# The last expert block's down matrices in three parts, and the overflow branch ahead of that block's last work

## The chip, the cores and the metric

The kernel runs on one NeuronCore of a Trainium2 chip. TensorE multiplies matrices and transposes, VectorE and ScalarE work elementwise, GpSimd gathers rows, SyncE issues most transfers; each has its own instruction stream, and they meet only at semaphores. Sixteen DMA engines move data between HBM and the on-chip memory. The metric is the time of one execution on the device in microseconds (us); smaller is better.

## The reference

Two transformer layers on 512 tokens of width 1024, in float32. Layer 0 has differential attention, layer 1 dilated attention over three groups. Each layer then has a mixture of experts, and this is what matters here: 32 experts in 4 groups, two experts for each token, each expert a gated network with a hidden width of 512.

```
g_idx = argmax(h @ w_group + b_group);  gates = g_w * softmax(top2 of the group's 8 experts)
expert(xb, e) = (silu(xb @ w_gate[e]) * (xb @ w_up[e])) @ w_down[e]
y[token] += gate * expert(h[token], e)
x = x + g_f * y
```

The gate and up matrices are 1024 x 512 and a down matrix is 512 x 1024, 2 MB each. Every expert's three matrices are read in both layers.

## The kernel before

After the routing, the (token, expert) pairs stand sorted into 14 blocks (NB) of 128 rows. Experts are ranked by load. The first blocks hold one expert each (WIDE), then come blocks that hold two experts of 64 rows (PAIRS) and blocks that hold four experts of 32 rows (FOURS). COLS says in which order the blocks are worked; the last one, block 13 in order, is a block of four experts. What doesn't fit in these rows would go through an overflow pass: a flag holds by how much an expert is overfull, and every engine branches on it. With this case's data the flag is zero and the pass is jumped over. Its code stands there all the same.

For a block p, TensorE does gate_up(p) (two products, each over 8 slices of the contraction), hidden_t(p) (four transposes of HIDDEN), down(p) and token_sums(p). In down(p) the product goes through two halves of the output columns (hf), and within each through 4 slices k of the contraction. For a block of four experts the four quarters run side by side in four column groups of the array, so 2 x 4 x 4 matmuls. A float32 matmul is two records in the trace, so they are 64 records. VectorE multiplies silu(gate) by up (hidden, L1497), copies the transposes (hidden_t, L1503), scales each half of the result into Y (y_out, L1519), and adds the token sums to x (add_sum, L1530). token_sums(p) (L2221) brings the rows of Y back to their tokens: eight matmuls of 128 x 512, for two halves and four chunks of tokens.

The order of the matrices is written out in MOE_ORDER: gate and up of a block, then down of the block before; for the last two blocks down of block 12, gate and up of block 13, down of block 13. SyncE issues them in that order, all on one queue (L529). Each goes to a fixed slot (8 slots in layer 0, 9 in layer 1), and SyncE first waits until the slot's last user is done. The slot's semaphore says when the matrix has arrived; TensorE waits for it in arrived().

At the end of a layer TensorE's order is: gate_up(13), hidden_t(13), down(13), the load of the flag and the branch (L2241), token_sums(13). VectorE's order is: pick, hidden, hidden_t and y_out of block 13, the flag and the branch (L1560), the eight additions. ScalarE branches at L995, GpSimd at L649, SyncE at L533, after the last down matrix is issued. Behind the additions of layer 0 follow the squares and the transposes of layer 1's attention, behind those of layer 1 the output.

Of the kernel before, what the change touches and what calls it, by code (L numbers as in the profile page):

```python
# [15 lines left out]
P = 128  # L16
# [209 lines left out]
def program(nc, t, const, masks, buckets, out):  # L226
    with ExitStack() as ctx:
# [193 lines left out]
        XR = [V[:, D * i:D * (i + 1)] for i in range(2)]  # L421
        HIDDEN, HIDDEN_T = V[:, 4 * D:4 * D + HALF], V[:, 4 * D + HALF:5 * D]
        Y = V[:, 5 * D:6 * D]
        PICK = [W[:, 2048:2560], W[:, 512:1024]]
        TOKENS = W[:, 2560:3072]

# [10 lines left out]
        def _(sp):  # L437
# [35 lines left out]
            for l in range(LAYERS):  # L473
                for n, (kind, layer, i) in enumerate(ORDER):
                    if layer != l or kind == "moe":
                        continue
                    if kind == "mod":
                        load(n, columns(t["kv_ada_w"], i - 12) if 12 <= i < 16 else
                             columns(t["ada_w"][i // 16], i % 16))
                    elif kind == "v":  # L480
                        load(n, columns(t["a_w_qkv"][0], 4 + i) if l == 0 else columns(t["kv_w"], GROUPS + i))
                    elif kind == "kq":
                        slot_free(n)
                        if l == 0:
                            parts = [(t["a_w_qkv"][0], D + 2 * P * i), (t["a_w_qkv"][0], 2 * P * i)]
                        else:
                            hh, g = divmod(i, GROUPS)
                            parts = [(t["kv_w"], g * HALF + hh * 2 * P), (t["b_w_q"][0], g * HALF + hh * 2 * P)]
                        for to, (w, at) in enumerate(parts):
                            sp.dma_start(slot(n)[:, 2048 * to:2048 * (to + 1)].rearrange("p (k n) -> p k n", k=KC),  # L490
                                         w[:, at:at + 2 * P].rearrange("(k p) n -> p k n", p=P)).then_inc(w_in[SLOT[n]], 16)
                    elif l == 0:
                        load(n, columns(t["a_w_o"][0], i))
                    else:
                        load(n, t["b_w_o"][0].rearrange("(k p) n -> p k n", p=P), k=4)

                m = AT["moe", l, 0]
                expert, ranked = {}, False
                for i, (p, kind, half) in enumerate(MOE_ORDER):  # L500
                    r = rank_of(p, half)
                    if r < FIXED:
                        expert[r] = r
                    elif kind == "g":
                        if not ranked:
                            sp.wait_ge(*sm[l]["eid_ready"](1))
                            ranked = True
                        expert[r] = sp.value_load(eid[0:1, r:r + 1], min_val=0, max_val=E - 1)
                    g, u, d = expert_weights(l, expert[r])
                    if l == 1 and i == 2:  # L510
                        sp.wait_ge(*sm[1]["qk_pe"](N_TILES))
                    elif l == 1 and i == 3:
                        sp.wait_ge(*sm[1]["s_pe"](N_STEPS))
                    elif l == 1 and i == 4:
                        sp.wait_ge(*sm[1]["pt_pe"](N_STEPS))
                    if i == 5:
                        sp.wait_ge(*sm[l]["gath"][0](16))
                    if SLOT[m + i] == RING and PREVIOUS[m + i] is None or l == 1 and i == 5:
                        if l == 0:
                            sp.wait_ge(t1_copy, 3)  # L520
                        sp.wait_ge(*sm[l]["xn_out"](16))
                        sp.wait_ge(*sm[l]["route_pe"](2))
                    elif (l, i) in ((0, 7), (1, 6)):
                        sp.wait_ge(*sm[l]["wo_pe"](2 * TC))
                    elif l == 1 and i == 7:
                        sp.wait_ge(*sm[1]["y_added"](2 * TC))
                        sp.wait_ge(*sm[1]["gate_pe"](2))
                    slot_free(m + i)
                    sp.dma_start(slot(m + i), {"g": g, "u": u, "d": d}[kind]).then_inc(w_in[SLOT[m + i]], 16)  # L529
                    if kind == "d":  # L530
                        del expert[r]

                most = sp.value_load(flag[0:1, 0:1], min_val=0, max_val=S)  # L533
                with sp.If(most > 0):
                    sp.wait_ge(*sm[l]["dn_pe"](2 * NB))
                    for b in range(OV_ROUNDS):
                        with sp.Fori(0, E) as e:
                            u0 = b * E
                            g, u, d = expert_weights(l, e)

                            sp.wait_ge(*ov[l]["dn_pe"](e + u0))
                            sp.dma_start(slot(0), g).then_inc(ov[l]["w"].sem, 16)
                            sp.dma_start(slot(1), u).then_inc(ov[l]["w"].sem, 16)
                            sp.dma_start(slot(2), d).then_inc(ov[l]["w"].sem, 16)
                    sp.wait_ge(*ov[l]["dn_pe"](OV_ROUNDS * E))
                    sp.wait_ge(*ov[l]["scat"](64 + 16 * OV_ROUNDS * E))
                    for c in range(TC):
                        if c:
                            sp.wait_ge(*ov[l]["hid"](OV_ROUNDS * E + c))
                        sp.dma_start(V[:, 0:2 * D].rearrange("p (k n) -> p k n", k=2), rows_of(l, c)).then_inc(ov[l]["w"].sem, 16)  # L550
                    sp.wait_ge(*ov[l]["hid"](OV_ROUNDS * E + TC))
# [461 lines left out]
        def _(dve):  # L1013
# [28 lines left out]
            for l in range(LAYERS):  # L1042
# [504 lines left out]
                y_out(NB - 2)  # L1547
                add_sums(NB - 2)
                pick(NB - 1)
                hidden(NB - 1)  # L1550
                hidden_t(NB - 1)
                y_out(NB - 1)

                def add_rows(c, signal, at):
                    step(dve.tensor_tensor(x3[:, c, :], x3[:, c, :], at[:, 0:D], ALU.add))
# [3 lines left out]

                most = dve.value_load(flag[0:1, 0:1], min_val=0, max_val=S)  # L1560
                with dve.If(most > 0):
                    for bb in range(OV_ROUNDS):
                        if bb:
                            dve.wait_ge(*o["tab_pe"](bb))
                        rows_at = ov_row[:, A * bb:A * (bb + 1)]
                        main_step, step = step, Steps(dve, o["step_dve"].sem)
                        step.base = bb if bb == 0 else bb + 2
                        step(dve.tensor_scalar(rows_at, over_by, float(-QP - P - P * bb), None, ALU.add))
                        if bb == 0:
                            step(dve.tensor_copy(OHW[:, :, 0:E], OHS))  # L1570
                            step(weigh(OHW, E))
                            dve.tensor_tensor(OHW[:, :, 0:E], OHW[:, :, 0:E], ids(E), ALU.mult)
                        step = main_step
                        for a in range(A):
                            at = 2048 + a * P
                            ins = dve.tensor_scalar(W[:, at:at + P], C[:, C_IOTA:C_IOTA + P], rows_at[:, a:a + 1], None, ALU.is_equal)
                        ins.then_inc(o["tab_f"].sem, 1)
                        dve.wait_ge(*o["tab_pe"](bb + 1))
                        cols = slice(bb * E, (bb + 1) * E)
                        main_step, step = step, Steps(dve, o["step_tab"].sem)  # L1580
                        step.base = 2 * bb
                        slot_table(bank[2][:, 0:2 * E], E, gate_ov[:, cols], dst_ov[:, cols], tok_ov[:, cols], o["tok"].sem, 3072 - 64)
                        step = main_step
# [18 lines left out]
                        add_rows(c, o["hid"].sem, V[:, 0:2 * D])  # L1602
                    dve.wait_ge(*o["hid"](OV_ROUNDS * E + TC))
                    step = main_step

                for c in range(TC):
# [16 lines left out]
        def _(pe):  # L1624
# [43 lines left out]
            for l in range(LAYERS):  # L1668
# [559 lines left out]
                for p in range(NB):  # L2228
# [4 lines left out]
                    elif p == NB - 2:  # L2233
                        down(p)
                        token_sums(p)
                        gate_up(p + 1)
                    else:
                        hidden_t(p)
                        down(p)

                most = pe.value_load(flag[0:1, 0:1], min_val=0, max_val=S)  # L2241
                with pe.If(most > 0):
                    pe.wait_ge(*s["y_evac"](2 * NB))
                    ohs = W[:, 0:4 * TC * E].rearrange("p (a n) -> p a n", n=2 * E)
                    for bb in range(OV_ROUNDS):
# [8 lines left out]
                    for bb in range(OV_ROUNDS):  # L2254
                        with pe.Fori(0, E) as e:
# [24 lines left out]
                                                    start=(k == 0), stop=(k == 3))  # L2280
                            ins.then_inc(o["dn_pe"].sem, 1)
                    pe.wait_ge(*o["y"](2 * OV_ROUNDS * E))

                token_sums(NB - 1)

# [31 lines left out]
```

## Time and profile before

| | us |
|---|---|
| three runs, median | 1838.29 |
| lowest, highest | 1838.28, 1844.95 |
| the profiled execution | 1839.16 |
| its span, first to last instruction | 1837.3 |
| TensorE busy | 1674.6 (91%) |
| VectorE busy | 653.2 (36%) |
| ScalarE busy | 371.1 (20%) |
| GpSimd busy | 55.3 (3%) |

A record is one instruction of one execution, in us from the span's start. PE is TensorE, PEld its loading of weights, DVE VectorE, ACT ScalarE, POOL GpSimd, SP SyncE; a q behind the name means the engine's sequencer. Busy time of a group counts overlapping records once. PEclk is the share of full clock that TensorE was granted: 1.00 is 2.4 GHz, 0.50 is 1.2 GHz.

### The profile page before, as it was taken

The page shows a single profiled execution, that of the slowest core. Times are in us where ns is not written, and L with a number is a line of the kernel's source. Part 1 is how long each engine was busy: PE and PEld are TensorE (multiplying, and loading weights), DVE is VectorE, ACT ScalarE, POOL GpSimd, SP SyncE. Part 2 cuts the span into 40 slices and gives each one's busy share as a digit, 9 for nine tenths or more (in the row PEclk, how much of TensorE's full clock was granted, in tenths as well). Part 3 has the DMA queues.
Part 4 walks back from the last instruction along what each step waited for, and adds up shares of the span by engine and source line. Part 5 has one row for each costly group of instructions (what it writes and reads, how often), then busy time and mean ns, then how long its engine had stood idle before and what let it go on. Part 6 is the DMA issues. An engine that isn't in the chain of part 4 may idle for free.

```text
span 1837.3 us, 18111 instructions
## 1 busy us (share of the span) xinstructions
PE 1674.6 (91%) x6904; PEld 732.1 (40%) x6904; DVE 653.2 (36%) x1400; ACT 371.1 (20%) x916; POOL 55.3 (3%) x61
## 2 busy tenths in 40 slices
PE   5999999988998997998699999998889989979995
PEld 2455555443332332332244455444433323323331
DVE  2576654350322322323376122224522322322331
ACT  3124344221111010010210143333311101001000
POOL 1000000210000000000000000001000000000000
PEclk9999998999999998999899999999999999989998
DMA  9962722149999999999666112021199999999995
GB/s 356 349 238 83 274 92 92 50 182 404 427 427 427 426 428 425 428 426 408 229 217 196 45 46 92 0 92 50 46 374 427 426 426 427 425 427 427 428 426 223
DMA packets 102524, 523.30 MB, mean 285 GB/s; under 512 B 6836, under 2 KB 44165, under 8 KB 77854
## 3 DMA queue, kind: packets, MB, share of 16 engines
q1 hardware_dynamic: 77632, 484.46, 64.6%
q0 software_dynamic: 7392, 19.99, 3.0%
q10 hardware_dynamic: 17406, 17.59, 3.0%
q8 instruction: 60, 0.98, 0.2%
q14 instruction: 34, 0.28, 0.0%
HBM read 521.98 MB, written 6.32 MB: 288 GB/s over the span
## 4 chain that ended last, share of the span: by engine, by line
PE 80%; DMA 11%; DVE 5%; issue 2%; ACT 1%; ACTq 0%; SPq 0%; DVEq 0%
PE psum L2177 19%; PE psum L2208 11%; PE psum L2221 10%; PE psum L1720 9%; PE psum L1928 9%; DMA ring<-in_moe_w_up_dram 6%; PE psum L1898 3%; PE psum L1775 3%; PE psum L2153 2%; DMA XN<-in_moe_w_up_dram 1%; DVE W L1077 1%; DMA XN<-in_moe_w_down_dram 1%; DMA HT<-in_moe_w_down_dram 1%; DMA V<-xn_scratch,tok 1%; PE psum L1749 1%
## 5 line engine op out<-in xcount | busy, mean ns | idle before, releaser
L2177 PE MATMUL psum<-ring,V 128*32 128x512 f32 (+2 forms) x1440 | 354.4, 619 | 31.0 <-DMA ring<-in_moe_w_up_dram 11.5
L2221 PE MATMUL psum<-V,W 128*128 128x512 f32 x448 | 220.3, 618 | 9.4 <-issue 4.6
L2208 PE MATMUL psum<-ring,V 128*64 128x512 f32 (+2 forms) x752 | 206.1, 609 | 20.7 <-DMA HT<-in_moe_w_down_dram 9.9
L2177 PEld LDWEIGHTS psum<-ring,V 128*32 128x32 f32 (+2 forms) x1440 | 118.6, 137 | 207.5 <-issue 201.1
L1530 DVE TENSOR_TENSOR X<-X,psum 128x512 f32<-128x512 f32 x224 | 153.7, 687 | 71.3 <-PE psum L2221 71.3
L972 ACT ACTIVATE V<-psum,modall,scls 128x128 f32<-128x128 f32 x216 | 81.1, 456 | 332.4 <-PE psum L2153 332.4
L1077 DVE SCALAR_TENSOR_TENSOR W<-ring,cact,W 128x512 f32<-128x512 f32 (+1 forms) x224 | 138.5, 618 | 7.7
L2221 PEld LDWEIGHTS psum<-V,W 128*128 128x128 f32 x448 | 73.0, 190 | 155.3 <-DVE X L1530 85.3
L2177 PE MATMUL psum<-XN,V 128*32 128x512 f32 (+2 forms) x240 | 112.6, 625 | 22.4 <-DMA ring<-in_moe_w_up_dram 22.1
L2177 PE MATMUL psum<-HT,V 128*32 128x512 f32 (+2 forms) x256 | 117.8, 615 | 3.5 <-DMA ring<-in_moe_w_up_dram 3.2
L1720 PE MATMUL psum<-HT,ring 128*128 128x512 f32 x256 | 117.2, 605 | 0.0
L1519 DVE SCALAR_TENSOR_TENSOR V<-psum,slot_gate,W 128x512 f32<-128x512 f32 x56 | 42.0, 751 | 207.3 <-PE psum L2208 207.3
L981 ACT ACTIVATE V<-psum 128x512 f32<-128x512 f32 x28 | 16.7, 597 | 486.3 <-PE psum L2186 405.2
L1497 DVE TENSOR_TENSOR V<-V,psum 128x512 f32<-128x512 f32 x28 | 19.2, 687 | 264.6 <-PE psum L2177 264.6
L2208 PEld LDWEIGHTS psum<-ring,V 128*64 128x64 f32 (+2 forms) x752 | 64.3, 138 | 121.4 <-issue 121.4
L1928 PE MATMUL psum<-HT,ring 128*128 128x512 f32 x192 | 88.8, 607 | 0.0
L1928 PE MATMUL psum<-ring 128*128 128x512 f32 x192 | 87.1, 596 | 0.0
L1503 DVE COPY V<-psum 128x512 f32<-128x512 f32 x28 | 19.4, 691 | 174.2 <-PE psum L2186 174.2
L1720 PEld LDWEIGHTS psum<-HT,ring 128*128 128x128 f32 x256 | 48.1, 193 | 56.2 <-issue 55.8
L1243 DVE SCALAR_TENSOR_TENSOR ring<-psum,colV,W 128x512 f32<-128x512 f32 x24 | 23.7, 989 | 112.5 <-ACT W L860 112.5
L2208 PE MATMUL psum<-XN,V 128*32 128x512 f32 (+1 forms) x128 | 61.2, 626 | 0.0
L1720 PE MATMUL psum<-ring,HT 128*128 128x512 f32 x128 | 59.1, 612 | 0.0
(313 smaller groups left out, 1822.7 us busy)
## 6 DMA issues: line engine op xcount, KB each, us to landing
ring<-in_moe_w_gate_dram SPq DMA_DIRECT2D x49, 2048.0 KB, 24.1
ring<-in_moe_w_down_dram SPq DMA_DIRECT2D x47, 2048.0 KB, 23.9
ring<-in_moe_w_up_dram SPq DMA_DIRECT2D x41, 2048.0 KB, 22.8
ring<-in_ada_w_dram SPq DMA_DIRECT2D x16, 2048.0 KB, 15.4
HT<-in_moe_w_up_dram SPq DMA_DIRECT2D x10, 2048.0 KB, 23.8
XN<-in_moe_w_gate_dram SPq DMA_DIRECT2D x9, 2048.0 KB, 21.7
XN<-in_moe_w_down_dram SPq DMA_DIRECT2D x8, 2048.0 KB, 21.6
ring<-in_ada_w_dram ACTq DMA_DIRECT2D x16, 1024.0 KB, 5.3
```

What stands on the lines that cost most here:

```text
L972: ins = act.activation(V[:, 2 * D + b * D + k * P:2 * D + b * D + (k + 1) * P], bank[0][:, q * P:(q + 1) * P], ACT.Identity, bias=mod[:, 2 ...
L1077: ins = dve.scalar_tensor_tensor(acc, w[:, k, :], cact[:, k:k + 1], acc, ALU.mult, ALU.add)
L1519: dve.scalar_tensor_tensor(Y[:, cols], bank[6 + hf], slot_gate[:, COLS[p]:COLS[p] + 1], gf_row[:, cols], ALU.mult, ALU.mult).then_inc(s["y ...
L1530: return dve.tensor_tensor(x3[:, c, cols], x3[:, c, cols], sum_bank(p, hf, c), ALU.add)
L1720: ins = pe.matmul(bank[n % 2], rows, cols, start=(k == 0), stop=(k == KC - 1))
L1775: ins = pe.matmul(bank[WO_BANKS[0][u]], OT0[k][:, c * P:(c + 1) * P], w3[:, k, :], start=(k == 0), stop=(k == KC - 1))
L1898: ins = pe.matmul(bank[u % 4], rows, slot3(n)[:, k, :], start=(k == 0), stop=(k == KC - 1))
L1928: ins = pe.matmul(bank[n % 2], w[:, k, (hp % 2) * P:(hp % 2 + 1) * P], (HTQ if kind else ht3)[:, k, :], start=(k == 0), stop=(k == KC - 1))
L2153: ins = pe.transpose(to[:, q * P:(q + 1) * P], V[:, b * D + k * P:b * D + (k + 1) * P], ident)
L2177: ins = pe.matmul(bank[2 + 2 * i + b][half * w:(half + 1) * w, :], V[:, col:col + w], slot3(x)[:, k, :], start=(k == 0), stop=(k == KC - 1))
L2208: ins = pe.matmul(bank[6 + hf][half * w:(half + 1) * w, :], HIDDEN_T[:, col:col + w], slot3(x, 4)[:, k, hf * HALF:(hf + 1) * HALF], start= ...
L2221: pe.matmul(sum_bank(p, hf, c), PICK[p % 2][:, c * P:(c + 1) * P], Y[:, hf * HALF:(hf + 1) * HALF], start=True, stop=True).then_inc(s["sum ...
```

## The change

The down matrices of block 13 come in three parts: columns 0 to 2D of the slot (slices k = 0 and 1) of all four experts, then slice 2 of all four, then slice 3 of all four. The first parts signal the slots' semaphores, the others two new ones, d_rest. TensorE's new last_down does hidden_t, then eight matmuls of ones into bank 0 whose result nobody uses, waits for the transposed rows, and goes through the three parts; in each part both halves of the columns. Both halves are finished in the last part. The flag is loaded and the branch taken before last_down on TensorE, and before hidden, hidden_t and y_out of block 13 on VectorE; so these stand in both arms of the branch.

```diff
+        d_rest = [sem("d_rest0"), sem("d_rest1")]
+        LAST_DOWN = ((0, 1), (2,), (3,))
...
-                    sp.dma_start(slot(m + i), {"g": g, "u": u, "d": d}[kind]).then_inc(w_in[SLOT[m + i]], 16)
-                    if kind == "d":
+                    if kind == "d" and p == NB - 1:
+                        sp.dma_start(slot(m + i)[:, 0:2 * D], d[:, 0:2 * D]).then_inc(w_in[SLOT[m + i]], 16)
+                    else:
+                        sp.dma_start(slot(m + i), {"g": g, "u": u, "d": d}[kind]).then_inc(w_in[SLOT[m + i]], 16)
+                    if kind == "d" and p < NB - 1:
                         del expert[r]
+                for part, rest in enumerate(d_rest):
+                    cols = slice((2 + part) * D, (3 + part) * D)
+                    for half in range(halves(NB - 1)):
+                        n = m + MOE_AT[NB - 1, "d", half]
+                        d = expert_weights(l, expert[rank_of(NB - 1, half)])[2]
+                        sp.dma_start(slot(n)[:, cols], d[:, cols]).then_inc(rest, 16)
...
                 pick(NB - 1)
-                hidden(NB - 1)
-                hidden_t(NB - 1)
-                y_out(NB - 1)
+
+                def last_rows():
+                    hidden(NB - 1)
+                    hidden_t(NB - 1)
+                    y_out(NB - 1)
...
                 with dve.If(most > 0):
+                    last_rows()
...
+                with dve.Else():
+                    last_rows()
...
-                    else:
-                        hidden_t(p)
-                        down(p)
+
+                def last_down():
+
+                    p, n = NB - 1, halves(NB - 1)
+                    w = P // n
+                    hidden_t(p)
+                    for _ in range(8):
+                        pe.matmul(bank[0], ones, C[:, 0:512], start=True, stop=True)
+                    at = [m + MOE_AT[p, "d", half] for half in range(n)]
+                    pe.wait_ge(*s["hid_t"](p + 1))
+                    pe.wait_ge(*s["y_evac"](p * 2))
+                    for part, ks in enumerate(LAST_DOWN):
+                        if part == 0:
+                            for x in at:
+                                arrived(pe, x)
+                        else:
+                            pe.wait_ge(d_rest[part - 1], 16 * n * (l + 1))
+                        for hf in range(2):
+                            for k in ks:
+                                for half, x in enumerate(at):
+                                    col = k * P + half * w
+                                    ins = pe.matmul(bank[6 + hf][half * w:(half + 1) * w, :], HIDDEN_T[:, col:col + w],
+                                                    slot3(x, 4)[:, k, hf * HALF:(hf + 1) * HALF],
+                                                    start=(k == 0), stop=(k == 3))
+                            if part == 2:
+                                ins.then_inc(s["dn_pe"].sem, 1)
 
                 most = pe.value_load(flag[0:1, 0:1], min_val=0, max_val=S)
                 with pe.If(most > 0):
+                    last_down()
...
+                with pe.Else():
+                    last_down()
 
                 token_sums(NB - 1)
```

## Rows read from the trace of the kernel before

**Rows 1.** Waits, 1790 to 1838: who waited for whom: us in total, times, longest

```profile
PE psum L2208 <- DMA XN<-in_moe_w_down_dram: 9.7, 1, 9.7
PE psum L2177 <- DMA ring<-in_moe_w_up_dram: 3.2, 1, 3.2
```

**Rows 2.** Chain of waits, end of layer 1: start, us, what

```profile
1792.29 21.61 DMA XN<-in_moe_w_down_dram
...
1814.40 8.97 PE psum L2208 x64
...
1824.97 7.12 PE psum L2221 x16
```

**Rows 3.** Waits, 850 to 900

```profile
PE psum L2208 <- DMA HT<-in_moe_w_down_dram: 9.9, 1, 9.9
...
PE psum L2221 <- issue: 4.6, 1, 4.6
```

**Rows 4.** Timeline, end of layer 0: start, us, engine line op, what, count [idle before]

```profile
856.14 0.81 SPq L529 DMA_DIRECT2D ring<-in_moe_w_down_dram  x2
...
859.36 8.59 PE L2177 MATMUL psum<-ring,V 128*32 128x512 f32 x64 [3.28 <-DMA ring<-in_moe_w_up_dram]
868.00 12.97 SPq L465 DMA_DIRECT2D ring<-in_kv_w_dram  x3
...
892.78 8.80 PE L2221 MATMUL psum<-V,W 128*128 128x512 f32 x16 [4.57 <-issue]
...
907.18 2.82 PE L1862 MATMUL psum<-C,XN 128*128 128x128 f32 x12 [5.59 <-DVE XN L1057]
```

**Rows 5.** Timeline, end of layer 1

```profile
1802.55 0.60 PE L2177 MATMUL psum<-ring,V 128*32 128x512 f32 x3
...
1804.03 0.66 PE L2186 MATMUL psum<-C,V 128*128 128x128 f32 x4 [0.88 <-DVE V L1497]
...
1818.42 0.61 PE L2208 MATMUL psum<-ring,V 128*32 128x512 f32 x3
...
1819.71 0.61 PE L2208 MATMUL psum<-ring,V 128*32 128x512 f32 x3
...
1820.03 0.75 DVE L1519 SCALAR_TENSOR_TENSOR V<-psum,slot_gate,W 128x512 f32<-128x512 f32 x1 [14.62 <-PE psum L2208]
...
1822.71 0.61 PE L2208 MATMUL psum<-ring,V 128*32 128x512 f32 x3
```

**Rows 6.** Instructions of L2241, both layers: count, ns min/median/max, first and last start

```profile
L2241 PEldq TENSOR_LOAD <-flag x2: 315/404/492, 885.5 to 1820.6; - x2
...
L2241 PEldq SEQ_ASSERT  x2: 18/23/28, 886.2 to 1821.2; - x2
```

**Rows 7.** DMA queues, 890.00 to 890.25: queue, kind: packets, MB, share

```profile
q8 instruction: 1, 0.02, 27.5%
```

**Rows 8.** DMA queues, 1822.25 to 1822.50

```profile
q8 instruction: 1, 0.02, 28.9%
```

**Rows 9.** Instructions of L995 (ScalarE's branch), 1780 to 1800

```profile
L995 ACTq SEQ_ASSERT  x1: 18/18/18, 1791.9 to 1791.9; - x1
```

**Rows 10.** DMA queues, 1795.5 to 1796.0

```profile
q14 instruction: 1, 0.01, 3.9%
```

**Rows 11.** DMA queues, 893.25 to 893.50

```profile
q8 instruction: 1, 0.02, 31.9%
```

**Rows 12.** Windows: stretch, length, busy of five engines, PEclk, DMA share, GB/s

```profile
1812.00:1813.00 1.00, 0.00 (x0) 0.00 (x0) 0.00 (x0) 0.00 (x0) 0.00 (x0) 0.50 0.19 82
...
1800.00:1805.00 5.00, 3.80 (x36) 1.19 (x28) 0.97 (x2) 0.00 (x0) 0.00 (x0) 1.00 1.01 433
887.00:888.00 1.00, 1.00 (x12) 0.14 (x4) 0.00 (x0) 0.00 (x0) 0.00 (x0) 1.00 1.05 387
893.00:894.00 1.00, 1.00 (x2) 0.39 (x2) 0.00 (x0) 0.00 (x0) 0.00 (x0) 0.59 0.90 307
895.00:900.00 5.00, 5.00 (x11) 2.20 (x10) 3.00 (x5) 0.16 (x1) 0.00 (x0) 0.84 0.01 2
```

## The prediction

> **What bounds the kernel now.** I read the chain of waits first: 80% of the span is TensorE. So what matters of the change is where it touches that chain, at the end of each layer's expert work. I then read the waits of those two stretches. In layer 1 TensorE sits 9.7 us in front of the last down products, until the last matrix lands, and 3.2 us in front of the up products [rows 1]. The chain of that tail [rows 2] is one piece after the other: transfer until 1813.9, down products from 1814.40, token sums from 1824.97, the last additions, output. Layer 0 looks the same, with a wait of 9.9 us, plus one that layer 1 has not: 4.6 us of "issue" ahead of the token sums [rows 3], where nothing that the profile names is late. The two timelines [rows 4, 5] give the places. The reader is to see that the last-landing transfer and the work behind it (9 us of down products, a branch, sums) stand in series in both layers.
>
> **Branch before the sums, as it is.** TensorE's sequencer loads the flag at 885.5 (layer 0) and 1820.6 (layer 1) [rows 6], 2.1 us before it starts its last down matmul (1822.71 in layer 1). The first sum starts at 892.78 and 1824.97 [rows 4, 2]. From load to first matmul: 7.3 us and 4.35 us. Why they differ shows in the instruction packets: the sequencer is ready at 886.2 and 1821.2 [rows 6]; the 16 KB packet of code follows at 890.0 and 1822.25 [rows 7, 8], so after 3.8 us and 1.0 us; the first matmul comes 2.7 us behind the packet in both. In layer 0 the transfer engines were full then (share 1.05, [rows 12]), in layer 1 empty. ScalarE's own branch in layer 1, taken at 1791.9 beside full engines [rows 9], has its packet at 1795.5, again 3.6 us [rows 10]. So a branch that needs a code block fetched costs 7.3 us beside full transfers and 4.35 us beside idle ones.
>
> **Part 1, the branch goes ahead of the last work.** Now the flag is loaded behind the last up matmul. That one starts at 859.36 + 8.59 - 0.59 = 867.36 in layer 0 and 1802.55 in layer 1 [rows 4, 5]. Less 2.1 us: loads at 865.3 and 1800.45. Both places lie inside the down transfers, with engines full (1.01, 433 GB/s, [rows 12]). I take 7.3 us for both; the other bound is 4.35 us. The first transposes of HIDDEN start at 872.6 and 1807.75. Without a branch they started at 1804.03 in layer 1 [rows 5], so 3.7 us are lost here, which would be hidden under the transfer if nothing followed. The other engines' branches: VectorE's moves behind the pick of block 13, some 18 us ahead of its next work; SyncE's stays last but follows 12 issues in place of 4, at about 0.42 us each (two took 0.81 us, [rows 4]), done by 861.2, while its next transfer waits until 868.00 anyway.
>
> **Part 2, eight warming matmuls.** They stand between the transposes and the wait for the matrices, of the same shape as the eight token sums (16 records of 128x512). Those took 7.12 us in layer 1 and 8.80 us in layer 0 [rows 2, 4], where TensorE had stood 4.6 us and the granted clock then fell to 1.2 GHz (0.59 in the second microsecond, [rows 12]). In the changed kernel TensorE stands 4.7 us, until 872.6 and 1807.75. So I take 8.8 us; with the clock kept it is 7.1. Behind 0.6 us of transposes they run 873.2 to 882.0 and 1808.35 to 1817.15.
>
> **Part 3, matrices in three parts.** The last byte comes no earlier. Four 2 MB transfers become four of 1 MB (8 KB per partition) and eight of 0.5 MB (4 KB), in one queue. The trace has full engines with 16 KB pieces at 433 GB/s and 2 KB pieces (layer 1's first weights) at 387 [rows 12]. Bounds for the last landing: 0 and 8.39 MB/387 - 8.39 MB/433 = 2.3 us later. I take 0.6 us, nearer the large pieces: 880.0 and 1815.0. Starvation is excluded: the pieces are issued faster (0.42 us) than they run (1.2 to 2.4 us). The first part, half the bytes, is in before 1806 and before 871. TensorE comes to it at 882.0 and 1817.15, when in layer 0 and in layer 1 all three parts have landed. Hence **no wait for a matrix is left: TensorE itself sets the end**, through the branch and the warming matmuls, and splitting the products gains only that they don't start cold.
>
> The products are 64 records in 16 passes of four; a pass at 2.4 GHz is (1822.71 - 1818.42)/10 = 0.43 us [rows 5], so 6.9 us in place of 8.97. They end at 888.9 and 1824.05. The first half of Y is ready only two passes before the end: its last matmul starts at 887.6, VectorE follows 0.3 us later and takes 0.75 [rows 5], done at 888.65. That is the one thing the split takes away (it used to be done 2.7 us before the end), and the last two passes still cover it. At 1.2 GHz it would be covered too.
>
> **Sum.** Layer 0: sums start at 888.9 in place of 892.78, 3.9 us earlier, and run warm, 7.1 in place of 8.8, 1.7 us more: 5.6 us. Layer 1: 1824.05 in place of 1824.97, 0.9 us. Behind the sums everything keeps its distance: in layer 0 the next transposes (907.18, waiting for VectorE) follow the additions, and the weights they meet are in since 895 (share 0.01, [rows 4, 12]). Layer 1 of the network starts 5.6 us earlier and ends 6.5 us earlier. The profiled execution took 1839.16 us: 1832.7. The median of the three runs shown, 1838.29, lies 0.9 us below it: 1831.8. I say 1832.
>
> Does each transfer cost something of its own? Five microseconds in which one down matrix ends and the next begins show 433 GB/s and share 1.01, with no hole [rows 12]. The Trainium skill (DMA: Bandwidth & Descriptors, "Bandwidth") asks for transfers of at least 1 MiB and its section on the anatomy of a DMA charges about 2.0 us for each. If that were paid in series, eight more would put the last landing 16 us later and the whole at some 1851; the trace does not agree, it shows such a cost only once, behind the last byte.
>
> **Rivals.**
> A, the fetch is cheap or the clock stays. If the branch costs 4.35 us, as beside idle transfers, layers 0 and 1 each start 2.95 us earlier; if the clock holds over the then shorter stand, 1.7 us more each. Both: 6.5 + 2 x 4.65 = 15.8, 1823. One of them: 1826 to 1829. For it: in layer 0 the last landing (880.0) would still be early enough, since the third part would be asked for at 882.5 at the earliest. Against: the two branches seen beside full engines, TensorE's and ScalarE's, waited 3.8 and 3.6 us for their packets. 25%.
> C, transfers pay by number. From the last bytes (within 1812 to 1813, [rows 12]) to the first product at 1814.40 pass about 1.6 us. Eight more transfers in series: 12.8 us, last landings at 892.2 and 1827.2. With 1.8 to 3.4 us of products behind them sums start at 894.0 and 1830.5, so 1.2 and 5.5 later, 1845. It decides from 8 us of delay on, for TensorE is not ready before. The full share above speaks against it. 4%.
> D, layer 0's gain is not passed on and only layer 1's 0.9 us stay: 1837.4. Against it the 12 us between the last weight's landing and its use. 7%.
> The forecast has the remaining 52%.
>
> **How the numbers follow.** The forecast's own spread is 1829 to 1835: 0.6 us of landing does nothing, the clock in one of the two layers does 1.7, runs differ by a microsecond. To hold 8 in 10 I go down to 1824, which leaves out only the fullest form of A, and up to 1839, which takes in D and the light half of B. What a measurement of this kernel can tell from no change is 0.5%, 9.2 us. Faster by more: most of A, and a forecast that errs by 3 us: 0.27. Slower by more: the heaviest B and what I don't see: 0.06. Within: 0.67.
>
> **What would show it.** In the changed profile: TensorE's flag load near 865 and 1800 minus the shift; its packet about 3.8 us behind; first transposes 7.3 us behind the load; 16 records of warming taking 8 to 9 us; no idle TensorE between them and the products; products 7 us, warm; sums directly behind, 7.1 us in both layers; the last landing earlier than the last part is asked for. It is wrong if TensorE waits again for a down matrix, if the load-to-transpose distance is under 5 us or over 9, or if a gap appears within the products.

## The result, and the profile after

| | before | after |
|---|---|---|
| median of 20 runs, us | 1840.40 | 1846.01 |
| lowest, highest | 1836.70, 1845.06 | 1841.63, 1848.29 |
| profiled execution, us (span) | 1839.16 (1837.3) | 1845.79 (1843.9) |
| first sum, layer 0 | 892.78 | 889.52 |
| last addition, layer 0 | 901.76 | 897.19 |
| block 13's hidden, layer 1 | 1803.28 | 1803.91 |
| first sum, layer 1 | 1824.97 | 1830.98 |

The ratio is 1.0029, interval 1.0020 to 1.0039: 5.3 us slower (3.7 to 7.2). 1832 with a range of 1824 to 1839 was forecast; the sign was wrong. Both profiles lie near their medians, so the 6.6 us between them can be followed through: layer 0 ends 4.6 us earlier, as forecast; the stretch from there to the end of layer 1 takes 5.2 us more (901.5 became 906.7); from hidden to the first sum of layer 1 are 27.1 us in place of 21.7, 5.4 more; the output 0.7 more.

**Layer 0** came as the sum had it. Timeline of TensorE and VectorE in the changed kernel (start, us; idle before and its releaser in brackets); the rows of before are [rows 4].

```profile
872.29 1.09 PE L2202 MATMUL psum<-C,V 128*128 128x128 f32 x4 [4.34 <-issue]
873.17 9.17 PE L2260 MATMUL psum<-C 128*128 128x512 f32 x16
...
889.52 7.11 PE L2237 MATMUL psum<-V,W 128*128 128x512 f32 x16 [0.18 <-DVE V L1530]
...
897.19 0.69 DVE L1541 TENSOR_TENSOR X<-X,psum 128x512 f32<-128x512 f32 x1 [0.35 <-issue]
```

The reader is to see the branch as "issue" (nothing that the profile names is waited for) ahead of the transposes (forecast 872.6), the sixteen slow records of warming (forecast 8.8 us), and sums that run at 2.4 GHz, 7.11 us for 8.80. The flag's load stands where it should, 7.1 us ahead of the first transpose:

```profile
L2280 PEldq TENSOR_LOAD <-flag x2: 315/403/491, 865.2 to 1801.0; - x2
```

**Layer 1** has the same pieces and one more. The chain of waits of the changed kernel (start, us, what); of before, [rows 2].

```profile
1796.70 7.11 PE psum L2193 x64
...
1803.91 0.70 DVE V L1508
1804.61 3.15 issue
1807.76 0.66 PE psum L2202 x2
1808.42 5.11 issue
1813.53 0.69 PE psum L2202 x2
1814.22 9.58 PE psum L2260 x16
1823.80 6.19 PE psum L2274 x56
...
1830.98 7.12 PE psum L2237 x16
```

The first "issue" is the branch. Then two records of transposes run, half of the four, and TensorE stands again for 5.11 us with nothing to wait for. In that time the next packet of its code travels; DMA queues of the changed kernel, 1810.75 to 1811.00:

```profile
q1 hardware_dynamic: 27, 0.10, 98.6%
q8 instruction: 1, 0.02, 27.2%
```

Read with e1 and e5 below: the branch landed a few records before the end of a code block, the next block was asked for only then, beside full transfers, and work resumed 2.6 us behind its packet, about the distance of [rows 7, 8] again. From there on the pieces are as forecast, and late. No down matrix is waited for: the waits of 1780 to 1850 hold no line with in_moe_w_down_dram.

**The middle.** Nothing of the change stands between 897 and 1795, and yet 5.2 us go there. Windows of 1240 to 1270, the end of layer 1's attention, where TensorE works in short pieces (the eighth figure is the granted clock): first before, then the changed kernel.

```profile
1240.00:1250.00 10.00, 6.92 (x49) 4.14 (x49) 3.63 (x11) 4.91 (x13) 0.00 (x0) 1.00 0.59 211
1250.00:1260.00 10.00, 7.38 (x92) 6.06 (x90) 7.73 (x25) 6.06 (x19) 4.92 (x5) 1.00 0.12 17
1260.00:1270.00 10.00, 7.65 (x34) 3.58 (x33) 2.50 (x4) 3.89 (x6) 0.00 (x0) 1.00 0.02 2
```

```profile
1240.00:1250.00 10.00, 6.91 (x60) 5.32 (x58) 4.45 (x18) 4.01 (x12) 0.00 (x0) 0.81 0.58 212
1250.00:1260.00 10.00, 7.65 (x70) 5.78 (x68) 7.67 (x22) 6.74 (x21) 4.91 (x5) 0.85 0.11 17
1260.00:1270.00 10.00, 8.34 (x29) 3.90 (x30) 1.53 (x3) 3.22 (x5) 0.00 (x0) 0.83 0.00 0
```

Before was granted 2.4 GHz throughout; the changed kernel does the same work partly at 1.2 GHz. (0.19 + 0.15 + 0.17) x 10 us = 5.1 us of clock missing, which is at most what it can cost here. It isn't the only place: from 900 to 910 the changed kernel was granted 0.66, the kernel before 0.84. Added up in such windows from 900 to 1330, the changed kernel spends 34 us at 1.2 GHz, the kernel before 20.

### The profile page after: what moved, and what is told of

It is laid out like the page before. It is cut to its first block, busy times and chain, and to the rows that moved or that the text cites. A ratio compares the mean times of both kernels' runs of the same rounds, so it can differ in the third digit from the quotient of the medians.

```text
span 1843.9 us, 18223 instructions
## 1 busy us (share of the span) xinstructions
PE 1695.1 (92%) x6936; PEld 743.1 (40%) x6936; DVE 653.4 (35%) x1400; ACT 371.5 (20%) x916; POOL 55.3 (3%) x61
## 4 chain that ended last, share of the span: by engine, by line
PE 80%; DMA 11%; DVE 5%; issue 2%; ACT 1%; SPq 1%; DVEq 0%
PE psum L2193 19%; PE psum L2224 10%; PE psum L1944 9%; PE psum L1736 9%; PE psum L2237 9%; DMA ring<-in_moe_w_up_dram 8%; PE psum L1914 3%; PE psum L1791 3%; PE psum L2169 2%; DMA XN<-in_moe_w_up_dram 1%; DVE W L1088 1%; DMA ring<-in_ada_w_dram 1%; PE psum L2049 1%; DMA V<-xn_scratch,tok 1%; PE psum L1765 1%
## 5 line engine op out<-in xcount | busy, mean ns | idle before, releaser
L2224 PE MATMUL psum<-ring,V 128*64 128x512 f32 (+2 forms) x672 | 188.3, 596 | 1.1 <-issue 1.0
L2193 PE MATMUL psum<-XN,V 128*32 128x512 f32 (+2 forms) x240 | 111.9, 621 | 21.1 <-DMA ring<-in_moe_w_up_dram 20.8
L1508 DVE TENSOR_TENSOR V<-V,psum 128x512 f32<-128x512 f32 x28 | 19.3, 688 | 264.1 <-PE psum L2193 264.1
L2224 PEld LDWEIGHTS psum<-ring,V 128*64 128x64 f32 (+2 forms) x672 | 59.4, 139 | 90.5 <-issue 90.5
L1944 PE MATMUL psum<-ring 128*128 128x512 f32 x192 | 87.0, 596 | 0.0
L1914 PE MATMUL psum<-ring 128*128 128x512 f32 x128 | 57.0, 598 | 0.0
```

What stands on the lines that cost most here:

```text
L1914: ins = pe.matmul(bank[u % 4], rows, slot3(n)[:, k, :], start=(k == 0), stop=(k == KC - 1))
L1944: ins = pe.matmul(bank[n % 2], w[:, k, (hp % 2) * P:(hp % 2 + 1) * P], (HTQ if kind else ht3)[:, k, :], start=(k == 0), stop=(k == KC - 1))
L2193: ins = pe.matmul(bank[2 + 2 * i + b][half * w:(half + 1) * w, :], V[:, col:col + w], slot3(x)[:, k, :], start=(k == 0), stop=(k == KC - 1))
L2224: ins = pe.matmul(bank[6 + hf][half * w:(half + 1) * w, :], HIDDEN_T[:, col:col + w], slot3(x, 4)[:, k, hf * HALF:(hf + 1) * HALF], start= ...
```

## The experiments

Two theories stood to be tested. **Landing**: the second stand in layer 1 made the change slow, and nothing else did. **Middle**: when layer 0 ends at another moment, other idle gaps of TensorE fall to 1.2 GHz, and some 5 us go that way in this kernel. The texts on record call them T and M; theory A in the later ones says that a delay costs its own length and nothing else. Each kernel below was compared with runs of the kernel before on the same chip; c1 is a single run. "Middle" is the distance in the profiled execution from the start of the last addition of layer 0 to hidden of block 13 in layer 1; "tail" that from there to the first sum.

| kernel | what it is | median, us | against before, us (interval) | last addition, layer 0 | middle | tail |
|---|---|---|---|---|---|---|
| before | | 1840.25 | | 901.76 | 901.5 | 21.7 |
| c1 | before once more | | | 902.09 | 901.7 | 21.5 |
| after | | 1846.01 | +5.3 (+3.7 to +7.2) | 897.19 | 906.7 | 27.1 |
| e1 | after, landing moved | 1840.27 | +0.2 (-2.4 to +2.6) | 896.60 | 906.5 | 21.1 |
| e2 | e1, branch late | 1833.03 | -7.9 (-11.4 to -4.4) | 895.08 | 905.0 | 16.8 |
| e3 | e1 without warming | 1829.34 | -11.6 (-16.0 to -7.4) | 891.41 | 907.0 | 15.0 |
| e4 | before, branch early | 1837.07 | -2.2 (-5.0 to +0.4) | 893.71 | 907.0 | 20.6 |
| e5 | e3, layer 0's gap filled | 1828.26 | -12.7 (-16.2 to -9.0) | 890.93 | 904.9 | 18.5 |
| e6 | before, held 1.1 us | 1845.69 | +6.6 (+4.0 to +9.0) | 901.61 | 907.8 | 21.9 |
| e7 | e3, branch between gate and up | 1823.81 | -17.3 (-21.0 to -13.6) | 887.94 | 905.8 | 15.3 |
| e8 | e7, held 2.2 us | 1822.38 | -15.3 (-19.3 to -11.4) | 891.79 | 902.1 | 14.6 |
| e9 | e7, layer 0's gap filled | 1820.74 | -18.9 (-21.3 to -16.4) | 892.26 | 900.1 | 14.7 |

The fourth column is the ratio of the comparison, less one, times the median of before on that chip (1840.40 for after, 1840.25 for e1 to e4, 1838.29 for e5 to e7, 1838.81 for e8 and e9). The last three are of one execution each. How far such an execution can stray shows in e7, e8 and e9: up to the first sum of layer 0 they hold the same code, and it starts at 880.24, 881.26 and 883.43.

**e1, the landing moved.** Records that never run, in the overflow arm, push the other arm along in the code:

```diff
                 with pe.If(most > 0):
+                    for _ in range(30):
+                        pe.matmul(bank[0], ones, C[:, 0:512], start=True, stop=True)
                     last_down()
```

> The changed kernel, with 30 matmuls (120 records) more in the overflow arm, which is never executed; all that changes is where TensorE's branch lands in its 16 KB code block. In the changed kernel's layer 1 two transposes run, then TensorE stands 5.1 us until the next code block is in. Theory T (landing): the stand goes, as 124 records are left behind the landing in place of some 4. Layer 1: transposes 1807.8 and all done, warming to 1817, products to 1824, sums at 1824.3 in place of 1830.98. So 6 to 7 us faster than the changed kernel in both theories. They part on the whole: T says that nothing but the stand made the change slow, so the gain of layer 0 (4.7 us) shows: some 7 us faster than before, 1833 to 1835 where before is 1840. Rival M (middle): between 902 and 1795 the changed kernel lost 8 us against before because what follows layer 0's earlier end doesn't keep up (other gaps get the slow clock), systematically; then this one is within 2 us of before.

(The middle's 8 us of this text are 5.2 by the profiles. And the padding stands in layer 0's arm too, whose code lies ahead of layer 1's, so how many records were left behind the landing isn't known from the edit.)

It came back to the time of before. The chain of e1's layer 1:

```profile
1803.75 3.05 issue
1806.80 1.09 PE psum L2202 x4
1807.88 9.04 PE psum L2260 x16
...
1824.10 7.12 PE psum L2237 x16
```

All four transposes run at once, no second stand, and the tail is 21.1 us for 27.1. So the second stand is worth 5.1 us by the ratios (1.0029 to 1.0001), 6.0 us in the profile: shown. But the theory that it was all fails: e1 ought to have been 7 us faster than before and is not. Layer 0 ends 5.2 us earlier, the tail is 0.6 us shorter, and the middle takes 4.9 us more.

**e2, the branch back behind the products.** last_down() and last_rows() stand once, ahead of the branches; parts and warming stay, and e1's padding too.

```diff
+                last_down()
                 most = pe.value_load(flag[0:1, 0:1], min_val=0, max_val=S)
                 with pe.If(most > 0):
-                    last_down()
...
-                with pe.Else():
-                    last_down()
```

> The changed kernel with the branches of TensorE and VectorE back behind the last products (three parts and warming kept; 120 unexecuted records in the overflow arm to keep the landing off a block's end). T: transposes at 868.8 and 1804.0, warming to 876.5 and 1811.7, products to 883.4 and 1818.6; then the branch, 7.3 us from load to sums in layer 0 and 4.35 in layer 1: sums at 888.6 and 1820.9 against 892.78 and 1824.97 before. 8 us faster than before. M: the layer 0 part (4 us) and more is lost again in the middle: within 2 us of before.

8 us faster than before, and so 8 us faster than e1, which differs in the place of the two branches alone (TensorE's and VectorE's). Where TensorE sets the end, the branch in front of the work costs more (7 us of fetching beside full transfers) than behind it (in layer 1 beside idle ones).

**e3, no warming.** The loop of eight matmuls is taken out of last_down, and 152 records stand in the overflow arm, to keep the landing clear of a block's end.

```diff
-                    for _ in range(8):
-                        pe.matmul(bank[0], ones, C[:, 0:512], start=True, stop=True)
```

> The changed kernel without the eight warming matmuls (and with 152 unexecuted records in the overflow arm, so that the landing is that of e1). T: the products begin behind the transposes at 874 and 1808.9, half of them at 1.2 GHz, and end with the last part: 882.5 and 1817.5. Sums 6.5 us earlier per layer than in e1, so 13 us faster than e1 and 18 to 20 faster than before: 1821. M: layer 0's share is lost, 7 us faster than e1. A rival W, that the warming pays for itself (products and sums cold without it): no faster than e1.

11 us faster than e1. Timeline of e3's TensorE in layer 1:

```profile
1802.27 0.63 PE L2202 MATMUL psum<-C,V 128*128 128x128 f32 x4 [4.04 <-issue]
1803.68 1.07 PE L2272 MATMUL psum<-ring,V 128*32 128x512 f32 x3 [0.78 <-DVE V L1514]
...
1813.38 7.11 PE L2237 MATMUL psum<-V,W 128*128 128x512 f32 x16
```

The products begin 1.4 us behind the transposes and take 9.7 us up to the sums, 2.5 us more than the changed kernel's 7.2 behind its warming, which had cost 9.0. Of these, 1.4 us are the slow clock (granted 0.86 over the 9.70) and 1.1 us a pause in the middle of a pass, which ends at 1807.89, 2.5 us behind a code packet at 1805.43: the landing wasn't quite that of e1. Rival W is out. The sum from the landing theory (18 to 20 us faster than before) is missed by the middle again, 907.0.

**e4, the early branch alone.** One transfer for each matrix, no warming, products half by half.

```diff
-        LAST_DOWN = ((0, 1), (2,), (3,))
+        LAST_DOWN = ((0, 1, 2, 3),)
...
-                            if part == 2:
+                            if True:
```

> The kernel before with the branch ahead of the last work alone: one transfer for each down matrix, products half by half, no warming (152 unexecuted records in the overflow arm). T: products start on arrival (879.4, 1814.4) as before and take 9 us cold, sums follow at once: 888.5 against 892.78 and warm (1.7 us less), 1823.5 against 1824.97. Some 7 us faster than before. M: within 2 us of before.

2.2 us faster, with an interval that just holds zero; 8 us earlier at the end of layer 0, and 5.4 us given back in the middle. Against e3 it also says what the three parts are worth: 9.4 us by the ratios, 7.7 by the medians. Its chain has the matrix and then all the products:

```profile
1790.43 22.27 DMA XN<-in_moe_w_down_dram
1812.71 0.14 issue
1812.84 8.51 PE psum L2263 x64
1821.35 7.08 PE psum L2228 x16
```

**c1, before once more.**

> The kernel before, unchanged, profiled a second time. From the last addition of layer 0 (901.65) to that of block 13's first VectorE work in layer 1 (1803.28) the first profile has 901.6 us; the changed kernel and the four variants have 905 to 907.5. Theory M (the middle loses 4 to 6 us whenever layer 0 ends earlier): 901 to 903 again, with about 20 us at 1.2 GHz between 900 and 1330. Rival L (the first profile was a lucky execution, the middle varies from run to run): somewhere else, 904 or more.

901.7 us, so two profiles of before agree, and the other five kernels' 905 to 907 stand apart from them. Both are of executions near the median, though (1839.2 and 1839.3). On this chip the runs of before go from 1836.1 to 1844.7 us, and the granted clock of the whole execution is 0.960 in the longest and 0.967 in the shortest: now and then before, too, loses some microseconds to the clock, and no profile shows where.

**e6, before, held back.** One more Square ahead of layer 1's first; it puts the real one 1.1 us later (899.12 to 900.21), not the 1.25 us that were expected.

```diff
                     junk = HT[:, 0:D] if l == 0 else W[:, 2048:2048 + D]
+                    if l == 1 and c == 0:
+                        act.activation(junk, x3[:, c, :], ACT.Square).then_inc(held, 1)
+                        act.wait_ge(held, 1)
```

> The kernel before with one more Square of 128x1024 on ScalarE (1.25 us) ahead of layer 1's first, which holds back the start of layer 1's attention by 1.25 us and changes nothing else. Additive theory A: 1.25 us slower than before, no more. Theory M in its clock form: which idle gaps of TensorE fall to 1.2 GHz depends on where they lie in time, so a shift of a microsecond can cost several: more than 3 us slower, with 29 us or more at 1.2 GHz between 900 and 1330 in place of 20.

**1.1 us of delay cost 6.6 us** (4.0 to 9.0), and theory A is out. The last addition of layer 0 starts at 901.61, as before; the tail is the same; the middle has 907.8. Part of the delay lies ahead of that addition, for VectorE first waits for a Square. A cleaner measure starts at layer 1's first transposes, behind the whole delay: from there to hidden are 896.1 us in before, 896.3 in c1 and 901.8 in e6, so 5.6 to 5.7 us are lost after the delay is over. Windows of e6:

```profile
1240.00:1250.00 10.00, 8.19 (x45) 4.53 (x43) 3.13 (x10) 4.25 (x13) 0.00 (x0) 1.00 0.56 200
1250.00:1260.00 10.00, 8.71 (x73) 7.24 (x72) 6.50 (x22) 5.73 (x20) 3.24 (x3) 0.66 0.03 12
1260.00:1270.00 10.00, 6.07 (x46) 3.92 (x45) 5.44 (x9) 3.86 (x6) 1.68 (x3) 0.88 0.12 17
```

This is the picture of the changed kernel, made from the kernel before by a delay alone. Over the whole stretch from 900 to 1330 the granted clock of before, and then of e6, is

```profile
900.00:1330.00 430.00, 403.08 (x1578) 203.20 (x1576) 177.28 (x431) 130.88 (x290) 9.42 (x8) 0.98 0.27 89
```

```profile
900.00:1330.00 430.00, 403.74 (x1554) 203.50 (x1553) 172.13 (x411) 130.05 (x288) 9.43 (x8) 0.96 0.27 89
```

that is some 20 us at 1.2 GHz against 34 (added up in windows of 10 us; the two decimals here leave 4 us either way).

**e5, the gap of layer 0's end filled.** Six matmuls of ones behind layer 0's token sums, into a bank that VectorE has read.

```diff
                 token_sums(NB - 1)
+                if l == 0:
+                    pe.wait_ge(*s["summed"](2 * TC * (NB - 1) + 1))
+                    for _ in range(6):
+                        pe.matmul(bank[2], ones, C[:, 0:512], start=True, stop=True)
```

> e3 with six matmuls of ones behind layer 0's last token sums, into a bank already read, so that TensorE stands 0.6 us in place of 5.8 before layer 1's first transposes. M (clock): the spell at 1.2 GHz at 895.1 to 901.9 goes, in which TensorE worked for 5.2 us, so 2.6 us are saved there; later spells may shift either way, so 0 to 6 us faster than e3. A: exactly 2.6 faster. If the clock has nothing to do with the middle's loss: no change from e3.

The middle fell by 2.1 us (904.9), near the 2.6 that theory A had for it, but the times (1 us apart, both intervals 7 to 9 us wide) don't tell it from nothing. The tail says why: 18.5 us for e3's 15.0. TensorE in layer 1, and the DMA queues from 1802.75 to 1803.00:

```profile
1799.76 0.63 PE L2202 MATMUL psum<-C,V 128*128 128x128 f32 x4 [4.11 <-issue]
...
1805.23 1.07 PE L2272 MATMUL psum<-ring,V 128*32 128x512 f32 x3 [2.13 <-issue]
```

```profile
q8 instruction: 1, 0.02, 27.1%
```

After the transposes and two passes of products TensorE stands for 2.13 us with nothing to wait for, a code packet travels, and work goes on 2.4 us behind it; the clock granted from there to 1810 is 0.50. The six matmuls lie ahead of layer 1's code and moved its landing nearer to a block's end. It is the changed kernel's second stand once more, brought in by an edit somewhere else, and with it e5 says nothing against the clock.

**e7, the branch where TensorE waits anyway.** The gate product is done, then the branch, then the up product in both arms.

```diff
-                        gate_up(p + 1)
+                        gate_up(p + 1, only=(0,))
...
                     w = P // n
+                    gate_up(p, only=(1,))
                     hidden_t(p)
```

> e3 with TensorE's branch between block 13's gate and up products, where TensorE waits for the up matrices anyway (both arms hold the up product too; the landing in the code block stays). In e3 the transposes stand 4.0 and 4.4 us behind hidden for the branch's sake. Here the flag is loaded 2.1 us before the gate product's end, the first up matmul comes 7.3 us later, so 5.2 us behind the gate product in place of 3.9 and 2.9: up products 1.3 and 2.3 us later, transposes 3.1 and 1.7 us earlier than in e3. If TensorE still sets the end, 3 and 1.7 us faster per layer than e3; if the last part's landing does by then, less. 0 to 5 us faster than e3.

5.5 us faster than e3, just above what was expected. Now the down matrices set the end at last; e7's chain:

```profile
1788.13 17.72 DMA XN<-in_moe_w_down_dram
...
1805.89 3.22 PE psum L2276 x16
1809.11 7.08 PE psum L2240 x16
```

Behind the last part only its sixteen records are left, which is what splitting along the contraction is for.

**e8 and e9, the best version.** e8 is e7 with two extra Squares as in e6; e9 is e7 with e5's six matmuls.

> e7, held back at the start of layer 1 by two extra Squares on ScalarE (2.5 us). e7 has the middle of the changed kernel (906 us from layer 0's last addition to block 13 in layer 1, three spells at 1.2 GHz at 1235, 1252 and 1262), the kernel before has 901.7 and one spell there. Additive theory A: 2.5 us slower than e7. Theory M in its clock form: the delay moves the idle gaps again; the loss may vanish, then the middle is 901.7 + 2.5 at most and the run 0 to 3 us faster than e7 in spite of the delay; or it stays, then 2.5 us slower. Either M outcome must agree with the spells in its profile.

> e7 with six matmuls of ones in TensorE's gap behind layer 0's last token sums, as e5 was to e3. e5 was 1 us faster than e3 by the medians, where the spell of its gap alone was worth 2.6. A: 2.6 us faster than e7. M: between 1 us slower and 5 us faster, by where the later gaps fall. This and e8 are the two candidates for the best version.

In e8 the loss of the middle vanished: 902.1 us, where e7 has 905.8. From layer 1's first transposes, behind the delay (2.2 us here), it is 896.6 for 900.5. Its windows (against 0.81 and 0.85 in the changed kernel):

```profile
1240.00:1250.00 10.00, 7.38 (x91) 6.06 (x92) 7.72 (x25) 6.06 (x19) 4.93 (x5) 1.00 0.12 18
1250.00:1260.00 10.00, 7.64 (x36) 3.87 (x35) 2.96 (x5) 3.90 (x6) 0.00 (x0) 1.00 0.02 1
```

So the delay did not make it slower beyond doubt: the medians put e8 1.4 us ahead of e7, the ratios 2 us behind, and the intervals overlap. e9 has the shortest middle of all, 900.1 us (894.8 from the first transposes), and is the fastest kernel run: 0.9897 of before (0.9884 to 0.9911), 1820.74 us, and by the ratios some 24 us faster than the changed kernel.

## Why the prediction was wrong

- **The branch's price** (7.3 us beside full transfers, for both layers): right. Load to first transpose is 7.1 us in layer 0 (865.2 to 872.29) and 6.8 in layer 1 (1801.0 to 1807.76). Rival A was wrong.
- **The warming matmuls** (8.8 us, and TensorE, not the matrices, sets the end): right, 9.2 and 9.6 us. The prediction saw that they take the place of the wait that the parts remove, and e3 confirms it: without them 11 us less.
- **The parts**: their last landing stayed ahead of TensorE's need; rival C was wrong. The landing was to come 0.6 us later. From the last up matrix's landing to the last down's are 20.5 us for 19.8 in layer 0, so 0.6 it was, but in layer 1 21.5 (1796.57 to 1818.12) for 19.5 (1794.38 to 1813.89), 2.0 us later and within the bound of 2.3; it cost nothing here, as TensorE came to it at 1823.8. The 2.0 us for each transfer that the prediction weighed stand in the Trainium skill (DMA: Bandwidth & Descriptors, "Anatomy of one DMA — SWDGE (gpsimd) path") for transfers that GpSimd issues; these are SyncE's. Products 7.1 us in layer 0 (882.27 to 889.35) where 6.9 stood, no gap in them.
- **Layer 0's 5.6 us**: 4.6 measured at its last addition. Of the missing 1.0 us, 0.6 stand ahead of the sums (889.52 for 888.9: warming 9.2 for 8.8, and VectorE's evacuation, which was not quite covered, 0.18 us of waiting), the rest in the additions.
- **Layer 1's landing** is the first step that failed. Rival B had the mechanism, the place and the order of size (up to 7.1 us in a layer; 5.1 measured, in one layer of two), but was given 12%, and the sum took the stand as zero. That was a choice between two things that the trace of before did not show. By e1 this is 5.1 us, and e5 brought a smaller one (2.1 us) back.
- **"Behind the sums everything keeps its distance"** is the second step that failed, and the sum rested on it. It looked for who waits for whom, found 12 us of slack for the weights, and took the clock of TensorE for a thing of the two tails alone. Rival D priced the loss of layer 0's gain at 1837.4 but named no mechanism. The runs show one, the clock: the middle takes 901.5 us in the kernel before, 6.2 us more with 1.1 us of delay (e6), and 3.3 to 5.4 us more in seven kernels whose layer 0 ends 4.6 to 13.8 us earlier. Only in e8 and e9 is the loss gone. In the changed kernel it is 5.2 us and ate layer 0's 4.6 whole.

With both steps put in, the sum has the right sign and over half of the size: -6.5 + 5.1 + 5.2 = +3.8 us, where the medians show +5.6 and the two profiles +6.6. What is left of the profiles' distance, 2.8 us, is layer 0's missing 1.0, the output's 0.7, and 1.2 in layer 1's tail, where the transposes cut in two took 0.7 us more, the warming 0.8 and the products with their evacuation 0.3, and the branch 0.5 less.

What stays open: what in the chip decides which of the short idle gaps is followed by a spell at 1.2 GHz. The runs show that it changes when what comes before is shifted, and nothing finer. The moment by the profile's clock isn't it, as c1 and then e6 show:

```profile
907.50 2.82 PE L1862 MATMUL psum<-C,XN 128*128 128x128 f32 x12 [5.58 <-DVE XN L1057]
```

```profile
907.54 2.82 PE L1866 MATMUL psum<-C,XN 128*128 128x128 f32 x12 [6.67 <-DVE XN L1061]
```

Both begin layer 1 at the same time, e6 after a longer gap, and e6 takes 5.6 us more from there. Nor is it always the stretch of 1240 to 1270: e3 and e4 have part of their loss from 970 to 1010 (granted 0.93 and 0.96, before 1.00). That the missing clock is the middle's whole loss is argued from such windows, not shown by a run that changes the clock alone. Nor was the place of the landing read from the code itself; it was inferred from e1, in which only records that never run were added, and from e5.

## What to carry to other kernels

A branch of TensorE is no cheap instruction: 4.4 to 7 us until the next matmul, and 2 to 5 us more if it lands near the end of a code block, which an edit of the code ahead of it can bring about (e5). Put it where the engine waits anyway (e7), and test a change with some unexecuted records more, to see whether its time hangs on the landing. When products are split so that little is left behind the last transfer, take out the warming that stood in for the wait, or the wait is only renamed. And where a kernel has stretches of short idle gaps, a gain of a few microseconds in front of them isn't sure to arrive: hold the stretch back by a microsecond once (e6), and see what the time does, before explaining a result of that size by the edit.

## What the runs showed of the hardware

- A delay of 1.1 us in one engine made the execution 6.6 us longer (4.0 to 9.0); the clock granted to TensorE was lower in stretches up to 350 us later (0.66 from 1250 to 1260, in before 1.00). With a delay of 2.2 us, e8 had a middle 3.7 us shorter than e7's.
- After a branch beside full transfers, the packet of the code block behind the one landed in starts 3.1 to 3.2 us after work resumes (1807.76 to 1810.93 in the changed kernel, 1799.76 to 1802.84 in e5), and work goes on 2.4 to 2.6 us behind the packet. That was a stand of 5.1 us where two transposes stood in between, and of 2.1 us with two passes of products more.
- Transfers of 0.5 MB in a queue cost little, but not nothing. In the changed kernel their last ones moved 410 GB/s, where the 2 MB ones moved 433 ([rows 12]), and the very last landed 3.2 us behind the one before it, where they otherwise follow at 1.3. In e7 to e9, where that landing sets the end of layer 1, it comes 21.4 to 21.6 us after the last up matrix's, for 19.5 in before. No run tried fewer parts with e7's branch. The row of the changed kernel:

```profile
1812.00:1814.00 2.00, 0.47 (x2) 0.47 (x3) 0.00 (x0) 0.00 (x0) 0.00 (x0) 0.50 1.03 410
```
